# A two-layer recurrent decoder step on one core: an earlier start of the weight loads, and an output tail turned tile by tile

## What is computed

```python
for l in range(DEPTH):
    hdn = rmsnorm(x, ns[0])
    x = x + 0.5 * rmsnorm(swiglu(hdn, ...[0]), ns[1])
    hdn = rmsnorm(x, ns[2])
    mix, st_new = token_mixers(hdn, pos, p, st, chunk)
    x = x + rmsnorm(mix, ns[3])
    hdn = rmsnorm(x, ns[4])
    x = x + 0.5 * rmsnorm(swiglu(hdn, ...[1]), ns[5])
return x, stacked_states
```

## Time and profile before

| what | value |
|---|---|
| runs | 1803.3, 1806.53, 1808.39 us; median 1806.53 |
| profiled execution, first to last instruction | 1796.3 us |
| what the median has around that span | 10.2 us (by the lowest run 7.0, by the highest 12.1) |
| TensorE busy | 1592.9 us, 89% of the span |
| VectorE / ScalarE / POOL busy | 50% / 31% / 9% |
| DMA | 194.17 MB, 108 GB/s over the span |
| mean granted TensorE clock | 0.871 of full |

### The profile page before, as it was taken

How to read it: one execution, slowest core, us unless ns; L and a number is a source line. 1 busy time by engine, 2 the same in 40 slices (tenths; PEclk the granted TensorE clock), 3 DMA queues, 4 the chain that set the end, 5 groups by cost and what they waited for, 6 DMA issues and landing times.

```text
span 1796.3 us, 28795 instructions
## 1 busy us (share of the span) xinstructions
PE 1592.9 (89%) x10846; PEld 1492.3 (83%) x10846; DVE 903.6 (50%) x1415; ACT 556.7 (31%) x752; POOL 164.9 (9%) x249
## 2 busy tenths in 40 slices
PE   4999989988787789999889999899788888899995
PEld 3999979977775679999879999799687757799994
DVE  4455455645454555553455544566363544655433
ACT  3333344440011143333353333454200111533331
POOL 6000000100133320000000000001002413000000
PEclk9999999988755589999989999899695556899997
DMA  8455443430011144554334545254101102255440
GB/s 194 149 166 164 159 136 116 148 101 1 3 30 33 12 115 139 164 164 139 117 121 163 164 152 176 71 165 129 48 1 26 26 14 64 95 163 163 142 163 27
DMA packets 184921, 194.17 MB, mean 108 GB/s; under 512 B 7284, under 2 KB 181700, under 8 KB 184688
## 3 DMA queue, kind: packets, MB, share of 16 engines
q1 hardware_dynamic: 176864, 178.27, 30.7%
q0 software_dynamic: 7376, 10.91, 3.5%
q10 hardware_dynamic: 576, 3.59, 0.5%
HBM read 186.55 MB, written 6.19 MB: 107 GB/s over the span
## 4 chain that ended last, share of the span: by engine, by line
PE 84%; DVE 7%; issue 5%; ACT 2%; DMA 1%; DVEq 0%; ACTq 0%; SPq 0%; POOL 0%
PE ps L468 82%; PE ps L471 2%; DVE y L1253 1%; DVE ring_r L1212 1%; DMA ring<-in_ffn_w_up 1%; DMA big<-in_x_sample 1%; DVE y L1670 0%; DVE arena L1483 0%; DVE x L1254 0%; ACT lnr L967 0%; DVE big L1590 0%; DVE big L1709 0%; ACT rrow L968 0%; DVE y L1227 0%; DVE Sbd L1552 0%
## 5 line engine op out<-in xcount | busy, mean ns | idle before, releaser
L1212 DVE TENSOR_TENSOR ring_r<-ring,whigh_r 128x2048 fp32r<-128x2048 f32 (+1 forms) x174 | 389.9, 2242 | 466.4 <-ACT whigh_r L945 466.1
L945 ACT ACTIVATE whigh_r<-ring 128x2048 fp32r<-128x2048 f32 (+1 forms) x174 | 326.2, 1875 | 481.6 <-PE ps L468 471.8
L468 PE MATMUL ps<-hdn,whigh_r 128*128 128x288 f32 x2016 | 328.4, 305 | 24.7 <-ACT hdn L955 15.0
L468 PEld LDWEIGHTS ps<-hdn,whigh_r 128*128 128x128 f32 x2016 | 292.3, 192 | 37.1 <-issue 31.8
L468 PE MATMUL ps<-hdn,ring_r 128*128 128x288 f32 x2016 | 315.9, 300 | 0.0
L468 PE MATMUL ps<-y_r,whigh_r 128*128 128x288 f32 x1888 | 293.4, 299 | 0.0
L468 PEld LDWEIGHTS ps<-hdn,ring_r 128*128 128x128 f32 x2016 | 288.1, 193 | 0.0
L468 PEld LDWEIGHTS ps<-y_r,whigh_r 128*128 128x128 f32 x1888 | 268.8, 191 | 0.0
L468 PE MATMUL ps<-big_r,whigh_r 128*128 128x288 f32 x832 | 130.4, 298 | 7.5 <-DVE arena_r L1212 7.5
L468 PEld LDWEIGHTS ps<-big_r,whigh_r 128*128 128x128 f32 x832 | 117.4, 190 | 8.5 <-issue 8.3
L468 PE MATMUL ps<-big_r,ring_r 128*128 128x288 f32 x704 | 110.9, 299 | 0.0
(11 more groups left out here) (328 smaller groups left out, 1624.4 us busy)
## 6 DMA issues: line engine op xcount, KB each, us to landing
ring<-in_ffn_w_gate SPq DMA_DIRECT2D x44, 1024.0 KB, 5.2
ring<-in_ffn_w_up SPq DMA_DIRECT2D x44, 1024.0 KB, 5.2
ring<-in_ffn_w_down SPq DMA_DIRECT2D x32, 1024.0 KB, 5.1
ring<-in_w_in SPq DMA_DIRECT2D x30, 1024.0 KB, 5.0
ring<-in_ffn_w_down SPq DMA_DIRECT2D x16, 768.0 KB, 4.4
ring<-in_w_out SPq DMA_DIRECT2D x8, 1024.0 KB, 5.4
cst<-in_const ACTq DMA_DIRECT2D x1, 2301.0 KB, 8.3
big<-in_x_prompt ACTq DMA_DIRECT2D x1, 1024.0 KB, 11.4
```

Of the source, the lines that this page charges most:

```text
L468: return pe.matmul(out, lhsT, rhs, start=start, stop=stop, **k)
L945: A(whighR[:, pos % 2, 0:rows * 256], ring[:, s, 0:rows * 256], ACT.Copy)\
L1212: return TT(out, in_, high, ALU.subtract)
```

## The change

At the start:

- ACT's first load takes only the first 256 columns of the constants (identity and ones) with a semaphore of its own, then x and the gains as before. Then ACT waits until x has landed and starts the load of the other 4346 columns.
- TensorE turns x after the identity and x. It waits for the other constants before the first norm's sums; VectorE waits for them before its loop over the layers, POOL before its own loop.
- SP no longer waits for x before the weights.

At the end:

- TensorE turns slice k of x for all three chunks as soon as that slice's update is there, into six PSUM banks (2c for columns 0 to 511 of chunk c, 2c+1 for the others), with no wait for copies.
- After slice 3, ScalarE copies the three left halves. After slice 7, ScalarE copies the right half of chunk 1, VectorE those of chunks 0 and 2.
- SP stores six half rows, the left ones first, instead of POOL's three whole ones.

```diff
+FIRST_CONST = CONST_AT["bdones"][0]
 @@ sync
-            sp.wait_ge(sem("x_loaded"), 32)
...
+            yp = O["y_prompt"].rearrange("o (c p) d -> c p (o d)", p=P)
+            out = (yp[0], yp[1], O["y_sample"].rearrange("b t d -> (b t) d"))
+            for c in range(3):
+                sp.wait_ge(sem("x_out_left"), c + 1)
+                sp.dma_start(out[c][:, 0:512], xtok_s[0:CH[c][1], c, 0:512]).then_inc(sem("y_stored"), 16)
+            for c, (ready, n) in enumerate((("x_out_even", 1), ("x_out_odd", 1), ("x_out_even", 2))):
+                sp.wait_ge(sem(ready), n)
+                sp.dma_start(out[c][:, 512:], xtok_s[0:CH[c][1], c, 512:]).then_inc(sem("y_stored"), 16)
+            sp.wait_ge(sem("y_stored"), 96)
 @@ tensor
-            pe.wait_ge(sem("const_loaded"), 16)
+            pe.wait_ge(sem("ident_loaded"), 16)
             pe.wait_ge(sem("x_loaded"), 32)
...
             pe.wait_ge(sem("x_done"), KT)
+            pe.wait_ge(sem("const_loaded"), 16)
...
-            pe.wait_ge(sem("x_done"), 24 * DEPTH + KT)
-            for c, (o, L) in enumerate(CH):
-                if c:
-                    pe.wait_ge(sem("x_out_read"), c)
-                for k in range(KT):
-                    g = tr(ps[0:L, k // 4, (k % 4) * P:(k % 4 + 1) * P], x[:, k, o:o + L])
+            for k in range(KT):
+                pe.wait_ge(sem("x_done"), 24 * DEPTH + k + 1)
+                for c, (o, L) in enumerate(CH):
+                    g = tr(ps[0:L, 2 * c + k // 4, (k % 4) * P:(k % 4 + 1) * P], x[:, k, o:o + L])
                 g.then_inc(sem("x_back"), 1)
 @@ scalar
-            act.dma_start(cst[:, :], I["const"]).then_inc(sem("const_loaded"), 16)
+            act.dma_start(cst[:, 0:FIRST_CONST], I["const"][:, 0:FIRST_CONST]).then_inc(sem("ident_loaded"), 16)
...
+            act.wait_ge(sem("x_loaded"), 32)
+            act.dma_start(cst[:, FIRST_CONST:], I["const"][:, FIRST_CONST:]).then_inc(sem("const_loaded"), 16)
...
+            act.wait_ge(sem("x_back"), KT // 2)
+            for c, (o, L) in enumerate(CH):
+                A(xtok_s[0:L, c, 0:512], ps[0:L, 2 * c, :], ACT.Copy).then_inc(sem("x_out_left"), 1)
+            act.wait_ge(sem("x_back"), KT)
+            A(xtok_s[:, 1, 512:], ps[:, 3, :], ACT.Copy).then_inc(sem("x_out_odd"), 1)
 @@ vector
+            dve.wait_ge(sem("const_loaded"), 16)
...
-            for c, (o, L) in enumerate(CH):
-                dve.wait_ge(sem("x_back"), c + 1)
-                for n in range(2):
-                    g = CP(xtok_s[0:L, c, 512 * n:512 * n + 512], ps[0:L, n, :])
-                g.then_inc(sem("x_out_read"), 1)
+            dve.wait_ge(sem("x_back"), KT)
+            for c in (0, 2):
+                L = CH[c][1]
+                CP(xtok_s[0:L, c, 512:], ps[0:L, 2 * c + 1, :]).then_inc(sem("x_out_even"), 1)
 @@ gpsimd
+            pool.wait_ge(sem("const_loaded"), 16)
...
-            for c in range(3):
-                pool.wait_ge(sem("x_out_read"), c + 1)
-                dma(yp[c] if c < 2 else ys, xtok_s[0:CH[c][1], c, :]).then_inc(sem("y_stored"), 16)
-
-            pool.wait_ge(sem("y_stored"), 48)
```

More of the change, by code:

```diff
@@ L1842, in _ @@
                 pool.sem_inc(sem("layers_stored"), 1)
-            yp = O["y_prompt"].rearrange("o (c p) d -> c p (o d)", p=P)
-            ys = O["y_sample"].rearrange("b t d -> (b t) d")
-            for c in range(3):
-                pool.wait_ge(sem("x_out_read"), c + 1)
-                dma(yp[c] if c < 2 else ys, xtok_s[0:CH[c][1], c, :]).then_inc(sem("y_stored"), 16)
-            pool.wait_ge(sem("y_stored"), 48)
 _INS = ["x_prompt", "x_sample", "state_ret", "state_ssm", "state_ssm_conv", "state_gdn", "state_gdn_conv",
```

## The result

| | before | changed kernel |
|---|---|---|
| median of the runs on one chip | 1805.39 us (4 runs, 1803.3 to 1808.39) | 1779.06 us (4 runs, 1778.2 to 1786.56) |
| ratio, 95% interval | | 0.987 [0.9845, 0.9894] |
| span of the profiled execution | 1796.3 us | 1778.3 us |
| start of the first norm's logarithm | 36.66 | 30.80 |
| end of the last update of x | 1778.37 | 1773.16 |

The change is faster, and by more than forecast: 1779.06 us lies under the range of 1786 to 1800. In a second group the same kernel gave 0.9864 [0.9849, 0.9879]. Its eight runs have a mean of 1780.2; the 72 runs of the kernel before, beside all groups, have 1803.3 (1794.36 to 1810.38; the groups' own means lie between 1802.9 and 1804.3). That is 23 us where 14.5 were forecast.

The account below looks back on a forecast made before the run. TensorE was taken as busy 89% of the 1796.3 us span, with only the two ends movable: 7.0 us at the start plus 7.5 at the end make 14.5, span 1781.8, with 10.2 around it 1792.0 us; range 1786 to 1800.

Parts of the forecast that it names:

- The end's term: After the last update of x: the last store lands 7.5 us earlier, bounds 6.2 to 8.1.
- The end, step by step: Working for the kernel's end: turns and left copies hide under updates, last landing at 1783.3 instead of 1790.8.
- The start's term: Up to the first product: the norm's last sum at 29.7 against 36.64, 7.0 us gained, bounds -2 to +10.
- They land at about 18.5: At the start: the rest of the constants, loaded behind x, lands at about 18.5 us.
- My estimate of 1 us behind the issue: At the start: the constants' first packet comes 1 us behind their issue, at some 9.3 us.
- the sum's second candidate: First norm's last sum bound by the constants: their landing + 8.4 us for all 16 sums, giving 26.9.
- The sharing, one packet each in turn: At the start: two queues sharing the DMA engines get about one packet each in turn; x lands at about 8.
- The 10.2 us that the median has around the span: Whole kernel: 10.2 us added to the forecast span of 1781.8 to give 1792.0 us.
- equal shares: Rival, start: weights take half the engines' time, constants land at 27 to 31, whole about 1800 us; chance 0.17.
- The slow stretch is the price: Rival, 19 to 30 us: data missing at 19 costs 7 us per MB; start gives 5, 1794 us; chance 0.20.
- The stores change nothing: Rival, end: the 5.5 us after the last landing grow behind SP's six stores, eating half the gain; 1796; chance 0.08.
- Slower: Rival, start: constants land last, at 42, behind all four ring loads; 1812.8 us; chance 0.03.

Follow-up runs that it names:

- e3: Changed kernel with its six half-row stores, and the wait for them, moved from SP to POOL: 1788.99 us, 0.992 of the kernel before.
- e4: Kernel before with its three whole-row last stores, and the wait for them, given to SP instead of POOL: 1798.71 us, 0.9976 of before.
- e12: Changed kernel with SP's six stores kept, but POOL instead of SP waits at the end until they land: 1782.35 us, 0.9882 of before.
- e8: Changed kernel with TensorE's and VectorE's wait for the rest of the constants moved behind the first block, to the mixers: 1772.23 us, 0.9828 of before.
- e11: e8 with both additions, e9's wait of SP for the identity and e10's constants loaded by POOL: 1771.59 us, 0.9821 of before.
- e2: Kernel before with only the end's part of the change: 1792.2 us, 0.9941 of before.
- e1: Kernel before with only the start's part of the change: 1791.68 us, 0.9933 of before.
- e13: e1 run once more, to settle the size of the start's share: 1792.32 us, 0.9956 of before.
- e14: Kernel before without SP's wait for x ahead of the weights, nothing else changed: 1804.24 us, 1.0016 of before.
- e15: e1 with SP's wait for x kept, so only the constants move behind x: 1810.53 us, 1.0046 of before.
- e6: Changed kernel without ACT's wait for x, so the rest of the constants queues right behind x and the gains: 1788.99 us, 0.9918 of before.
- e7: Changed kernel with SP's third weight load held back until the constants have landed: 1782.93 us, 0.9894 of before.
- e10: e8 with the rest of the constants loaded by POOL behind the fourth ring load: 1772.21 us, 0.9834 of before.
- e9: e8 with SP's first load held until the identity has landed: 1790.37 us, 0.9907 of before.

## Why the prediction was wrong

**The direction and the two places were right**; both ends gained. From profile to profile the span fell 18.0: 5.9 at the first product, 12.8 at the end, the middle 0.7 longer. The gain was 8.6 us larger than forecast (23.1 and 14.5).

1. *The end's term, 7.5 us, was mis-sized: it measured 12.8, far outside the 6.2 to 8.1 that it was given.* The step that failed is "The end, step by step", which put the last landing 7.5 us earlier and carried the 5.5 us behind it over unchanged. They were in the text (1796.3 - 1790.8), but only as something that might grow behind SP's stores. e3, e4 and e12 show that they go with POOL finishing last. The rest of the step was good: 2.57 us to the last issue (forecast 2.8), 2.1 to its landing (2.2), 1.54 for ScalarE's left copies (1.8), 0.60 for a copy of 512 columns (0.6). The last three turns took 0.91 and not 0.74. From last update to last landing it was 12.4 us before (1790.8 - 1778.37) and is 4.7 now (1777.8 - 1773.16): 7.7, against the forecast 7.5. All that the sum lacked is the empty stretch, 5.5 before and 0.5 now.
2. *The start's term, 7.0 us, came out near its size by the trace (5.9 to the first product) by luck, through errors that cancel.* "They land at about 18.5" failed: the constants landed at 23.97. "My estimate of 1 us behind the issue" for their first packet had no row behind it and was 3.7; in that time the weights had the engines nearly to themselves. So the second ring load, said to be the bound with 22.2, was in at 14.3. The 5.5 us by which the constants were late are 1.9 of a later issue (x in at 10.17), 2.7 of that delay and 0.9 of a slower passage: 10.1 us from first packet to landing and not 9.2. (The sum's own terms add up to 18.1 and not 18.5.) The norm then was late by the constants, as in the sum's second candidate, but the 16 sums took 6.47 and not 8.4. e8 shows the wait's price, 6 us. The sharing, one packet each in turn, was right, and x at 10.17 against 8 is that rule plus a later first packet: x's first packets come just after 4, behind the weights' of 3 to 4 us (243 packets to 1); in e11, where SP waits, x lands 2.7 us sooner.
3. *Some 3 us are in the runs and not in the traces.* The 18 runs of the start alone give 10, where their norms are 6 to 7 sooner; 12.8 and 6 to 7 make 19 to 20 of 23. The stretch from norm to norm differs by up to 9 us between profiled executions of kernels that have it in common (1733.2 in before, 1742.2 in e2) with the granted clock (0.871 and 0.865). The runs list their clocks, and these go the same way: 0.8693 in the mean of the 18 runs of e1 and e13, 0.8665 in the 72 of before, 0.8662 and 0.8665 in e14 and e15, which gain nothing. By a straight line through the 72 runs of before, 0.0028 more clock goes with 3 us less. So the missing 3 us come with a higher clock under the changed start. The earlier norm as such is not what raises it, since e6 has 0.8706 with its norm at 36.24; what does stays open.
4. *The base.* "The 10.2 us that the median has around the span" do not exist: every later run lists its span, and the run's own time is 1.5 to 1.6 us above it, before's as well. The profiled execution of before, some 1797.9 us, was one of the fastest: 8 of 72 runs were under 1798. Taking the gain off the median was right, but the median of three runs was 3.2 us above the mean of the 72. So of the 11.8 us between 1792.0 and the changed kernel's mean, 3.2 are the base, 5.3 the end, and 3.3 the start together with the clock of item 3.

Of the rivals, *equal shares* fell by the packet counts, although its sign (TensorE waits for `cst`) came: that sign didn't separate it from late constants. *The slow stretch is the price* is half right: what is missing when it begins is dear (e6, e14, e15), but the changed kernel's second load was in before it. *The stores change nothing* had the right stretch and the wrong direction. *Slower* did not happen, and e15 shows that it can, by another way: weights and not constants last.

## What to carry to other kernels

Look at what the span has behind the last landing; if nothing moves there, see which engine waits for the last stores, and let SP wait and not POOL (4.9 us here, from e12's end to the changed kernel's). When two loads share the DMA engines, count rows, not bytes: each queue got one row per turn here, so a load with rows of 1 KB starved beside a table with rows of 17 KB (4.9% against 88.6% of the engines' time), and it must be through before that table is issued. And put each wait at the first instruction that reads the data: the wait for the whole table ahead of the first block cost 6 us here.

## What the runs showed of the hardware beside that

- POOL as the last engine to finish leaves 5 to 6 us of empty span behind the last landing (5.5, 5.8 and 5.3 us in before, e3 and e12), SP 0.4 to 0.5 (e4 and the changed kernel).
- Two edits of the start, worth nothing (1.0016 [0.9997, 1.0035]) and a loss (1.0046 [1.0027, 1.0064]) alone, make a gain together (0.9956 [0.9936, 0.9976]).
- The same table of 2173 KB came at 0.37 MB/us between 9 and 14 us (e6), and at 0.28 between 15 and 20 (e7), with more of the engines' time in its packets (88% and 96%). Whether weights were beside it from 15 to 20 made no difference (1.41 MB in e7 and in the changed kernel).
- A load issued just behind one of the other hardware queue has its first packet late: x on ACT's queue 2.5 us behind its issue at 1.55, the weights in e14 more than 4 us behind theirs at 1.38, the constants 3.7 us in the changed kernel, 2.3 in e7 and 0.9 in e15, where SP had issued nothing yet. x landed 2.3 to 2.7 us sooner in e11, where SP held back, than in e10 and the changed kernel, and 1.6 sooner in e9 than in e8.
